# A 31-tap depthwise convolution bounced through DRAM: written and read back in pairs of chunks, run five chunks behind its gates, with weight unit 5 loaded after it

## The chip, the cores and the metric

The kernel runs on one core of a Trainium2 chip. The metric is the device time of one execution in microseconds (us). All times below are from one profiled execution of the kernel before the change, or from its three timed runs.

## What is computed

Two small transformer stacks run one after the other on 256 tokens of width 1024: the first has a convolution block, an attention block and two MLPs, the second two attention blocks and two gated MLPs. Only the convolution block of the first stack is touched:

```python
def conformer_conv(h, w_pw1, b_pw1, w_dw, b_dw, ln_g, ln_b, w_pw2, b_pw2):
    u = h @ w_pw1 + b_pw1
    a, gate = jnp.split(u, 2, axis=-1)
    u = a * jax.nn.sigmoid(gate)
    u = jnp.pad(u, ((0, 0), (CONV_WIDTH - 1, 0), (0, 0)))
    u = lax.conv_general_dilated(u, w_dw[:, None, :], window_strides=(1,), padding='VALID',
                                 dimension_numbers=('NWC', 'WIO', 'NWC'),
                                 feature_group_count=D_MODEL) + b_dw
    u = jax.nn.silu(layer_norm(u, ln_g, ln_b))
    return u @ w_pw2 + b_pw2
```

Everything after it (`h = h + rms_norm(m)`, the MLP, and all later layers) depends on its result.

## The kernel before, in words

Features lie on the 128 partitions, so the width of 1024 is eight chunks of 128 features by 256 tokens. Every float32 product is made of three float16 ones (high by high, low by high, high by low). Weights come from DRAM in units of 2 MB (4096 float32 per partition) into two buffers, `staged` 0 and 1, even units in the one, odd units in the other. A unit has two halves. ScalarE (ACT) makes the high part of a half (`split`, line 1460, `w_hi`), then VectorE (DVE) the low part (`split`, line 2124, `w_lo`); a half is numbered g, so unit u has g = 2u and 2u + 1. The semaphore `lo_split` counts the halves done. Units 0 to 3 are pw1, 4 and 5 pw2, 6 to 13 the first MLP's first matrix. SyncE (SP) issues every load in a written order; a unit may be loaded once both halves of the unit two before it are split.

The convolution block runs as follows.

- **Gates.** TensorE (PE) makes for each chunk j two products of pw1, the value and the gate (`glu_chunk`, lines 678 to 680, 48 matmuls of 256 columns). They lie in pairs of PSUM banks. Banks 0 and 1 serve chunks 0, 3, 5 and 7, banks 2 and 3 serve 1, 4 and 6, and banks 4 and 5 chunk 2 alone; so chunk 5 may start only when DVE has drained chunk 3, chunk 6 when it has drained chunk 4, chunk 7 after chunk 5. DVE drains with `late_pair` (line 2380), builds packed taps (line 2387), makes the gated value (line 2400) and its low part (line 2404), and after chunks 0 to 3 splits one half of a unit of weights (line 2124). ACT makes the sigmoid (line 1631) and the high part (line 1637).
- **Bounce.** The convolution packs four taps into the contraction. For that, the gated chunk (high and low part side by side, 576 float16 per partition) is written to DRAM (`write_glu`, line 623) and read back four times, each time shifted by one more element, to other partitions (`spread_glu`, line 633: four DMAs of 143 KB, rows of 572 elements). Four buffers hold shifted chunks, two in `qT` and two in `kT`.
- **Convolution.** `conv_chunk` (line 959) is 96 matmuls with 32-column weights for each chunk. Chunk j - CONV_LAG is convolved after the gates of chunk j. ACT takes the result out (`conv_out`, line 1622).
- **Layer norm.** PE sums the chunks (`mean`, line 966), DVE subtracts the mean (line 2414), ACT squares (line 1652), PE sums by token (line 734), ACT takes the root (line 1654), DVE inverts (line 2417), and so on to SiLU and the parts of pw2's input.
- **pw2.** PE makes eight products in four banks. DVE drains each, squares it and adds the square (lines 2228, 2207, 2217; `into_m`), and splits halves 12 and 13 between them; ACT splits halves 12 to 14. When all eight are summed, PE forms the sum by token (line 734), the norm's root follows (line 1498), and the first MLP can begin.

SP's order in this part before the change: unit 2, unit 3, then for each chunk c the write of chunk c + 1 and the four reads of chunk c, with unit 4 behind the reads of chunk 4, unit 5 behind those of chunk 5, and units 6 and 7, the constants and the positions at the end.

Of the kernel before, what the change touches and what calls it, by code (L numbers as in the profile page):

```python
# [31 lines left out]
P = 128  # L32
# [18 lines left out]
CONV_LAG = 4  # L51
# [246 lines left out]
def conformer_mla_fox_dsa_moba_kernel(nc, w_stream, vec_dram, const_dram, x_dram, pos_dram, out_dram):  # L298
    with ExitStack() as ctx:
# [59 lines left out]
        def pack_weights(b):  # L359
# [6 lines left out]
        U_SIZE = PACK * U_ROW  # L366
        shifted = [b[:].rearrange("p c t -> p (c t)").bitcast(F16)[:, U_SIZE * i:U_SIZE * (i + 1)].rearrange(
            "p (r h t) -> p r h t", r=PACK, h=2) for b in (qT, kT) for i in range(2)]
        u_rows = nc.dram_tensor("u_rows", (DC, P, U_ROW), F16, kind="Internal").ap()
# [43 lines left out]
        u_shifted = [sem(f"u_shifted_{b}") for b in range(U_RING)]  # L413
# [171 lines left out]
        def _(sp):  # L585
# [34 lines left out]
            def write_glu(c):  # L620

                sp.wait_ge(u_lo_ready, c + 1)
                sp.dma_start(u_rows[c], glu_parts[:, c % U_RING, :, :].rearrange("p h t -> p (h t)")).then_inc(
                    u_written[c % 2], 16)

            def spread_glu(c):

                sp.wait_ge(u_written[c % 2], 16 * (c // 2 + 1))
                if c >= U_RING:
                    sp.wait_ge(conv_product, c - U_RING + 1)  # L630
                by_group = u_rows[c].rearrange("(r c) n -> c r n", r=PACK)
                for j in range(PACK):
                    sp.dma_start(shifted[c % U_RING].rearrange("p r h t -> p r (h t)")[CPART * j:CPART * j + CPART, :,
                                                                                       0:U_ROW - PACK],
                                 by_group[:, :, j:j + U_ROW - PACK]).then_inc(u_shifted[c % U_RING], 16)
# [7 lines left out]
            write_glu(0)  # L643
            for c in range(DC):
                if c + 1 < DC:
                    write_glu(c + 1)
                spread_glu(c)
                if c in (4, 5):
                    early_unit(c)
# [17 lines left out]
        def _(pe):  # L667
# [275 lines left out]
            def conv_chunk(c):  # L943

                b = 4 + c % 3
                pe.wait_ge(u_shifted[c % U_RING], SHIFTED * (c // U_RING + 1))
# [7 lines left out]
                u = shifted[c % U_RING]  # L954
# [499 lines left out]
        def _(act):  # L1454
# [172 lines left out]
            for j in range(DC):  # L1627
# [6 lines left out]
                if j >= U_RING:  # L1634

                    act.wait_ge(u_shifted[j - U_RING], SHIFTED)
# [8 lines left out]
            for c in range(DC - CONV_LAG - 1, DC):  # L1645
                if c < DC - 1:
                    split(2 * FIRST["pw2"] + c - (DC - CONV_LAG - 1))
# [1314 lines left out]
```

## Time and profile before

| | us |
|---|---|
| three timed runs, median (lowest, highest) | 1207.9 (1207.46, 1215.44) |
| the profiled execution, its own time | 1205.27 |
| its span (first to last instruction) | 1203.3 |
| PE busy | 1154.8 |
| DVE busy | 849.2 |
| ACT busy | 671.8 |

The span lies 2 us inside the execution's own time. The stages that the change touches lie between 28 and 124 us of the span; what follows them is some 1080 us in which PE is busy nearly all the time. A busy PE is not PE at its peak, since matmuls overlap: the time from one start to the next (0.11 us for 256 columns) counts, not the duration of one (0.27 us).

### The profile page before, as it was taken

How to read it: one execution, taken by the hardware profiler on the slowest of the kernel's cores; microseconds unless marked ns; L12 is line 12 of the kernel's file. 1: busy time of each engine (PE TensorE's matmuls, PEld its weight loads, DVE VectorE, ACT ScalarE, POOL GpSimd, SP SyncE). 2: the span in 40 equal slices, each digit the busy share in tenths (PEclk: the TensorE clock that was granted, in tenths of full speed). 3: DMA queues.
4: the chain of work that ended last, by engine and by line, in shares of the span. 5: the costliest groups of instructions: out<-in, count | busy, mean ns of one | idle time of the engine just before them, and what ended most of it. 6: DMA issues, size and time to landing. Idle time of an engine off the chain costs nothing.

```text
span 1203.3 us, 26382 instructions
## 1 busy us (share of the span) xinstructions
PE 1154.8 (96%) x10544; PEld 987.7 (82%) x10544; DVE 849.2 (71%) x1403; ACT 671.8 (56%) x1034; POOL 213.6 (18%) x166
## 2 busy tenths in 40 slices
PE   9989999999889999999999999999999999999997
PEld 7878788888767888888877678888887777888886
DVE  5846786754865877555687468888677665888775
ACT  6445576433656466533565476665655656666542
POOL 0000000000002000000031433554231333355400
PEclk9998999999999999999999999999999999999999
DMA  8592365555251355555232435554565334455352
GB/s 335 156 321 79 117 243 191 196 209 209 79 202 71 141 211 209 210 205 193 91 115 97 152 128 183 217 214 147 166 249 189 120 108 181 155 216 207 139 197 78
DMA packets 22394, 208.37 MB, mean 173 GB/s; under 512 B 2480, under 2 KB 9008, under 8 KB 9136
## 3 DMA queue, kind: packets, MB, share of 16 engines
q1 hardware_dynamic: 22320, 207.32, 47.9%
q8 instruction: 53, 0.87, 0.3%
q14 instruction: 21, 0.17, 0.0%
HBM read 205.09 MB, written 2.23 MB: 172 GB/s over the span
## 4 chain that ended last, share of the span: by engine, by line
PE 52%; issue 17%; DVE 12%; POOL 6%; ACT 6%; DMA 5%; SPq 0%; POOLq 0%; DVEq 0%; ACTq 0%
PE ps L678 12%; PE ps L680 12%; PE ps L679 12%; POOL tmp L2054 5%; DMA staged<-weights 5%; DVE w_lo L2124 4%; ACT w_hi L1460 2%; PE ps L959 2%; POOL probs L2063 1%; PE ps L689 1%; PE ps L691 1%; PE ps L690 1%; PE ps L862 1%; PE ps L734 1%; PE ps L885 1%
## 5 line engine op out<-in xcount | busy, mean ns | idle before, releaser
L1460 ACT ACTIVATE w_hi<-staged 128x2048 f16<-128x2048 f32 (+3 forms) x190 | 352.6, 1870 | 192.4 <-PE ps L680 149.6
L2124 DVE SCALAR_TENSOR_TENSOR w_lo<-staged,w_hi 128x2048 f16<-128x2048 f32 (+3 forms) x190 | 424.6, 2249 | 40.9 <-ACT w_hi L1460 40.7
L678 PE MATMUL ps<-f_hi,w_hi 128*128 128x256 f16 x1596 | 435.1, 273 | 5.8 <-ACT qT L1539 2.7
L679 PE MATMUL ps<-f_lo,w_hi 128*128 128x256 f16 x1596 | 435.0, 273 | 0.0
L680 PE MATMUL ps<-f_hi,w_lo 128*128 128x256 f16 x1596 | 435.0, 273 | 0.0
L678 PE MATMUL ps<-x_hi,w_hi 128*128 128x256 f16 x912 | 249.2, 273 | 4.4 <-DVE x_lo L2154 2.9
L680 PE MATMUL ps<-x_hi,w_lo 128*128 128x256 f16 x912 | 249.0, 273 | 0.0
L679 PE MATMUL ps<-x_lo,w_hi 128*128 128x256 f16 x912 | 248.9, 273 | 0.0
L678 PEld LDWEIGHTS ps<-f_hi,w_hi 128*128 128x128 f16 x1596 | 156.1, 98 | 26.7 <-issue 3.4
L679 PEld LDWEIGHTS ps<-f_lo,w_hi 128*128 128x128 f16 x1596 | 156.2, 98 | 18.4
L680 PEld LDWEIGHTS ps<-f_hi,w_lo 128*128 128x128 f16 x1596 | 156.2, 98 | 18.1
L2063 POOL TENSOR_TENSOR probs<-probs,peak 128x128 f32<-128x128 f32 x80 | 64.3, 833 | 485.0 <-DVE peak L2309 373.8
L2054 POOL TENSOR_TENSOR tmp<-tmp,stat 128x256 f32<-128x256 f32 x44 | 110.4, 2510 | 124.2 <-ACT tmp L1938 124.2
L678 PEld LDWEIGHTS ps<-x_hi,w_hi 128*128 128x128 f16 x912 | 89.7, 98 | 25.7 <-issue 8.4
L679 PEld LDWEIGHTS ps<-x_lo,w_hi 128*128 128x128 f16 x912 | 89.3, 98 | 12.1 <-issue 0.2
L680 PEld LDWEIGHTS ps<-x_hi,w_lo 128*128 128x128 f16 x912 | 89.3, 98 | 10.6
L2478 DVE TENSOR_SCALAR m<-ps 128x256 f32 (+1 forms) x16 | 6.8, 424 | 63.3 <-PE ps L680 54.4
L1922 ACT ACTIVATE tmp<-pad,vec 128x256 f32<-128x256 f32 x44 | 26.4, 599 | 38.0 <-DVE pad L2700 37.8
L2073 POOL TENSOR_TENSOR kT<-kT,stat 128x256 f32<-128x256 f32 x5 | 5.0, 997 | 231.8 <-ACT kT L1800 231.8
L2453 DVE SCALAR_TENSOR_TENSOR tmp<-ps,stat 128x256 f32<-128x256 f32 x64 | 26.6, 418 | 22.9 <-PE ps L680 21.9
L689 PE MATMUL ps<-x_hi,w_hi 128*128 128x256 f16 x144 | 39.4, 273 | 2.0 <-DVE x_lo L2148 2.0
L691 PE MATMUL ps<-x_hi,w_lo 128*128 128x256 f16 x144 | 39.2, 273 | 0.0
(309 smaller groups left out, 1586.5 us busy)
## 6 DMA issues: line engine op xcount, KB each, us to landing
staged<-weights SPq DMA_DIRECT2D x81, 2048.0 KB, 8.1
staged<-weights SPq DMA_DIRECT2D x16, 1408.0 KB, 6.2
staged<-weights SPq DMA_DIRECT2D x4, 1024.0 KB, 10.4
qT<-u_rows SPq DMA_DIRECT2D x16, 143.0 KB, 3.6
kT<-u_rows SPq DMA_DIRECT2D x16, 143.0 KB, 3.1
u_rows<-probs SPq DMA_DIRECT2D x8, 144.0 KB, 2.5
cst<-constants SPq DMA_DIRECT2D x1, 1031.5 KB, 9.7
h<-x_turned SPq DMA_DIRECT2D x1, 1024.0 KB, 7.3
```

Source lines behind the costliest of these rows:

```text
L678: pe.matmul(out, wh, xh[:, c, :], start=(c == 0), stop=False)
L679: pe.matmul(out, wh, xl[:, c, :], start=False, stop=False)
L680: last = pe.matmul(out, wl, xh[:, c, :], start=False, stop=(c == kc - 1))
L689: pe.matmul(out, wh, xh[:, c, :], start=(c == 0), stop=False)
L691: last = pe.matmul(out, wl, xh[:, c, :], start=False, stop=(c == kc - 1))
L959: last = pe.matmul(ps[CPART * r:CPART * r + CPART, b, 0:T], w[:, c, q, :, r], u[:, r, h, at], start=(q == 0 and n == 0), stop=(q == PACKS ...
L1460: act.activation(w_hi[:, s, o:o + n], staged[:, s, o:o + n], ACT.Copy, scale=SW).then_inc(hi_split, 1)
L1922: act.activation(tmp[:, j, :], pad[:, j, 0:T], ACT.Identity, bias=vec[:, bass.ds(i * 4 + (VCOL[f"b_cv_{layer}"] + n), 1)], scale=vec[:, ba ...
L2054: pool.tensor_tensor(tmp[:, j, :], tmp[:, j, :], LATE_SCALE, ALU.mult).then_inc(g_normed[layer], 1)
L2063: last = pool.tensor_tensor(probs[:, hd % 3, sl], probs[:, hd % 3, sl], peak[:, hd % 2, 6 + t:7 + t].to_broadcast([P, P * (t + 1)]), ALU.mult)
L2124: dve.scalar_tensor_tensor(w_lo[:, s, o:o + n], staged[:, s, o:o + n], SW, w_hi[:, s, o:o + n], ALU.mult, ALU.subtract).then_inc(lo_split, 1)
L2453: dve.scalar_tensor_tensor(tmp[:, n % 2, :], ps[:, hidden_bank(i, n), 0:T], 0.0, LATE_SCALE, ALU.max, ALU.mult).then_inc(drained[one], 1)
```

## The change

- One write carries two chunks, and one set of four reads carries two chunks, in rows twice as long (`PAIR_ROW`; reads of 1148 elements). There are two buffers, each of a pair, in place of four, each of a chunk.
- `CONV_LAG` is 5 in place of 4.
- Unit 4 is issued behind the reads of pair 1 (chunks 2 and 3), unit 5 behind the reads of pair 3 (the last).
- ACT writes over a gated chunk once the pair before in that place is written to DRAM; before, it waited until the chunk had been read back.
- ACT splits halves 8 and 9 between the takings-out of the convolution, half 10 after the last of them and ahead of the norm's squares, and half 11 ahead of pw2's halves 12 to 14. DVE splits half 10 after the mean is subtracted, and half 11 in `into_m` after the first product.

```diff
-CONV_LAG = 4
+CONV_LAG = 5
...
-        U_SIZE = PACK * U_ROW
-        shifted = [b[:].rearrange("p c t -> p (c t)").bitcast(F16)[:, U_SIZE * i:U_SIZE * (i + 1)].rearrange(
-            "p (r h t) -> p r h t", r=PACK, h=2) for b in (qT, kT) for i in range(2)]
-        u_rows = nc.dram_tensor("u_rows", (DC, P, U_ROW), F16, kind="Internal").ap()
+        PAIR_ROW = 2 * U_ROW
+        shifted = [b[:].rearrange("p c t -> p (c t)").bitcast(F16)[:, 0:PACK * PAIR_ROW].rearrange(
+            "p (r i h t) -> p r i h t", r=PACK, i=2, h=2) for b in (qT, kT)]
+        u_rows = nc.dram_tensor("u_rows", (DC // 2, P, PAIR_ROW), F16, kind="Internal").ap()
...
+            def write_glu(p):
+
+                sp.wait_ge(u_lo_ready, 2 * p + 2)
+                b = 2 * (p % 2)
+                sp.dma_start(u_rows[p], glu_parts[:, b:b + 2, :, :].rearrange("p b h t -> p (b h t)")).then_inc(
+                    u_written[p % 2], 16)
+
+            def spread_glu(p):
+
+                sp.wait_ge(u_written[p % 2], 16 * (p // 2 + 1))
+                if p >= 2:
+                    sp.wait_ge(conv_product, 2 * p - 2)
+                by_group = u_rows[p].rearrange("(r c) n -> c r n", r=PACK)
                 for j in range(PACK):
+                    sp.dma_start(shifted[p % 2].rearrange("p r i h t -> p r (i h t)")[CPART * j:CPART * j + CPART, :,
+                                                                                      0:PAIR_ROW - PACK],
+                                 by_group[:, :, j:j + PAIR_ROW - PACK]).then_inc(u_shifted[p % 2], 16)
...
-            write_glu(0)
-            for c in range(DC):
-                if c + 1 < DC:
-                    write_glu(c + 1)
-                spread_glu(c)
-                if c in (4, 5):
-                    early_unit(c)
+            for p in range(DC // 2):
+                write_glu(p)
+                spread_glu(p)
+                if p % 2:
+                    early_unit(4 + p // 2)
             early_unit(6)
             early_unit(7)
...
-                pe.wait_ge(u_shifted[c % U_RING], SHIFTED * (c // U_RING + 1))
+                pe.wait_ge(u_shifted[c // 2 % 2], SHIFTED * (c // 4 + 1))
...
-                    act.wait_ge(u_shifted[j - U_RING], SHIFTED)
+                    act.wait_ge(u_written[j // 2 % 2], 16)
...
             for c in range(DC - CONV_LAG - 1, DC):
-                if c < DC - 1:
-                    split(2 * FIRST["pw2"] + c - (DC - CONV_LAG - 1))
+                if c < 4:
+
+                    act.wait_ge(product["pw1"], 2 * c + 8)
+                    split(2 * FIRST["pw2"] + c - 2)
                 conv_out(c)
+            split(2 * FIRST["pw2"] + 2)
             root_next()
...
+            split(2 * FIRST["pw2"] + 3)
             behind("pw2")
...
+                    if name == "pw2" and n == 0:
+                        split(2 * u0 + 3)
                     if n % 2 and n < DC // 2:
                         split(2 * u0 + n // 2 + 4)
...
-            for g in range(4):
+            for g in range(2):
                 split(2 * FIRST["pw2"] + g)
...
+            split(2 * FIRST["pw2"] + 2)
             dve.wait_ge(ln_rooted, 1)
```

The change moves instructions on PE, ACT and DVE; three places follow, each first before the change and then with it (line numbers of the changed kernel are one to five off). A name in brackets is a semaphore that the row waits for.

The first is PE's row at the end of chunk 4's gates (678 to 680, in the changed kernel 677 to 679, are gates; 959, or 958, is the convolution). Before:

```order
L679 MATMUL ps<-x_lo,w_hi 128x256
L680 MATMUL ps<-x_hi,w_lo 128x256
L959 MATMUL ps<-qT,f_hi 32x256 [waits pw1_drained,pack_built,u_shifted_0]
L959 MATMUL ps<-qT,f_hi 32x256 x7
L959 MATMUL ps<-qT,f_lo 32x256 x4
```

And with the change:

```order
L678 MATMUL ps<-x_lo,w_hi 128x256
L679 MATMUL ps<-x_hi,w_lo 128x256
L677 MATMUL ps<-x_hi,w_hi 128x256 [waits pw1_drained,lo_split]
L678 MATMUL ps<-x_lo,w_hi 128x256
L679 MATMUL ps<-x_hi,w_lo 128x256
```

Where the convolution of chunk 0 stood, the gates of chunk 5 stand now; their first matmul waits for a drained bank and for a split half, and the convolution comes 48 matmuls later.

The second is ACT's row from the convolution's takings-out (1622, now 1621) to the norm's squares (1652, now 1654); 1460 (now 1459) is the high part of a half of weights. Before:

```order
L1622 ACTIVATE xn<-ps,vec 128x256 [waits conv_product]
L1460 ACTIVATE w_hi<-staged 128x2048 [waits landed_1]
L1622 ACTIVATE xn<-ps,vec 128x256 [waits conv_product]
L1460 ACTIVATE w_hi<-staged 128x2048 [waits landed_1]
L1622 ACTIVATE xn<-ps,vec 128x256 [waits conv_product] x2
L1528 ACT_TABLE_LOAD
L1528 ACTIVATE unused<-cst 128x1
L1652 ACTIVATE sq<-xn 128x256 [waits ln_centred] x8
```

And with the change:

```order
L1459 ACTIVATE w_hi<-staged 128x2048 [waits landed_0,pw1_product]
L1621 ACTIVATE xn<-ps,vec 128x256 [waits conv_product] x5
L1459 ACTIVATE w_hi<-staged 128x2048 [waits landed_1]
L1527 ACT_TABLE_LOAD
L1527 ACTIVATE unused<-cst 128x1
L1654 ACTIVATE sq<-xn 128x256 [waits ln_centred] x8
```

Half 10 has moved from between the takings-out to behind the last one, ahead of the table load and the squares.

The third is DVE's row at the start of `into_m`. Before (2228, 2207 and 2217 are drain, square and sum of one product, 2124 is the low part of a half):

```order
L2228 TENSOR_SCALAR m<-ps,vec 128x256
L2207 TENSOR_TENSOR sq<-m 128x256
L2217 TENSOR_TENSOR stat<-stat,sq 128x256
L2228 TENSOR_SCALAR m<-ps,vec 128x256
L2207 TENSOR_TENSOR sq<-m 128x256
L2217 TENSOR_TENSOR stat<-stat,sq 128x256
L2124 SCALAR_TENSOR_TENSOR w_lo<-staged,w_hi 128x2048
```

And with the change:

```order
L2231 TENSOR_SCALAR m<-ps,vec 128x256 [waits pw2_product,dve_step]
L2210 TENSOR_TENSOR sq<-m 128x256 [waits pw2_drained]
L2220 TENSOR_TENSOR stat<-stat,sq 128x256 [waits m_squared]
L2127 SCALAR_TENSOR_TENSOR w_lo<-staged,w_hi 128x2048 [waits hi_split]
L2231 TENSOR_SCALAR m<-ps,vec 128x256 [waits pw2_product]
L2210 TENSOR_TENSOR sq<-m 128x256 [waits pw2_drained]
L2220 TENSOR_TENSOR stat<-stat,sq 128x256 [waits m_added,m_squared]
L2127 SCALAR_TENSOR_TENSOR w_lo<-staged,w_hi 128x2048 [waits hi_split]
```

One half more (number 11) is split there, between the first product and the second; two others stand in both kernels.

## Rows read from the trace of the kernel before

**Rows 1.** The page, busy us, share of the span and instructions of an engine.

```profile
PE 1154.8 (96%) x10544; PEld 987.7 (82%) x10544; DVE 849.2 (71%) x1403; ACT 671.8 (56%) x1034; POOL 213.6 (18%) x166
```

**Rows 2.** Stretches (us): PE, PEld, DVE, ACT, POOL busy (instructions), PEclk, DMA share, GB/s.

```profile
72.00:74.00 2.00, 1.47 (x29) 1.32 (x32) 2.00 (x2) 0.00 (x0) 0.00 (x0) 0.50 0.91 330
74.00:76.00 2.00, 2.00 (x60) 1.89 (x53) 0.34 (x1) 0.44 (x1) 0.00 (x0) 0.70 0.92 174
...
69.70:78.50 8.80, 4.95 (x128) 4.43 (x127) 4.49 (x2) 4.43 (x5) 0.00 (x0) 0.81 0.77 245
...
41.30:44.10 2.80, 2.75 (x96) 2.55 (x96) 2.80 (x4) 1.55 (x2) 0.00 (x0) 1.00 0.64 180
```

**Rows 3.** Timeline of PE: start, duration (us), [idle before, releaser].

```profile
34.17 0.27 PE L678 MATMUL ps<-x_hi,w_hi 128*128 128x256 f16 x1 [0.32 <-DVE tmp L2380]
41.35 0.42 PE L959 MATMUL ps<-qT,f_hi 128*32 128x256 f16 x8 [1.78 <-DMA qT<-u_rows]
...
57.54 0.42 PE L959 MATMUL ps<-kT,f_hi 128*32 128x256 f16 x8
...
65.64 0.42 PE L959 MATMUL ps<-kT,f_hi 128*32 128x256 f16 x8
...
72.53 0.41 PE L959 MATMUL ps<-qT,f_hi 128*32 128x256 f16 x3 [2.88 <-issue]
...
78.94 0.41 PE L959 MATMUL ps<-qT,f_hi 128*32 128x256 f16 x7 [1.46 <-issue]
...
87.02 1.99 PE L966 MATMUL ps<-xn,cst 128*128 128x256 f32 x8
```

**Rows 4.** Timeline of DVE in the gates: drains of chunks 1, 3, 4; a split.

```profile
33.61 0.74 DVE L2380 TENSOR_TENSOR tmp<-ps,stat 128x256 f32<-128x256 f32 x2
...
41.00 2.28 DVE L2124 SCALAR_TENSOR_TENSOR w_lo<-staged,w_hi 128x2048 f16<-128x2048 f32 x1
43.21 0.74 DVE L2380 TENSOR_TENSOR tmp<-ps,stat 128x256 f32<-128x256 f32 x2
...
48.01 0.74 DVE L2380 TENSOR_TENSOR tmp<-ps,stat 128x256 f32<-128x256 f32 x2
```

**Rows 5.** DMA in stretches, KB each and us to landing.

```profile
u_rows<-probs SPq DMA_DIRECT2D x1, 144.0 KB, 1.7
...
u_rows<-probs SPq DMA_DIRECT2D x1, 144.0 KB, 8.9
...
staged<-weights SPq DMA_DIRECT2D x1, 2048.0 KB, 14.5
...
staged<-weights SPq DMA_DIRECT2D x1, 2048.0 KB, 8.0
...
q8 instruction: 1, 0.02, 6.9%
```

**Rows 6.** The page, DMA issues of the whole span, median us to landing.

```profile
kT<-u_rows SPq DMA_DIRECT2D x16, 143.0 KB, 3.1
```

**Rows 7.** Timeline of SP: the bounce's last write and last four reads.

```profile
68.13 0.34 SPq L623 DMA_DIRECT2D u_rows<-probs  x1
...
77.06 1.88 SPq L633 DMA_DIRECT2D kT<-u_rows  x4
```

**Rows 8.** Timeline of ACT behind the convolution's last taking-out.

```profile
87.64 1.28 ACT L1528 ACT_TABLE_LOAD   x1
...
89.51 2.73 ACT L1652 ACTIVATE sq<-xn 128x256 f32<-128x256 f32 x8 [0.38 <-DVE xn L2414]
...
107.24 1.91 ACT L1460 ACTIVATE w_hi<-staged 128x2048 f16<-128x2048 f32 x1 [3.48 <-PE ps L691]
```

**Rows 9.** Timelines of DVE and PE in pw2: first drain, last sum, PE behind it.

```profile
106.98 0.48 DVE L2228 TENSOR_SCALAR m<-ps,vec 128x256 f32<-128x256 f32 x1 [2.47 <-PE ps L691]
...
120.24 0.43 DVE L2217 TENSOR_TENSOR stat<-stat,sq 128x256 f32<-128x256 f32 x1
...
120.81 0.58 PE L734 MATMUL ps<-cst,stat 128*128 128x1 f32 x4 [0.19 <-DVE stat L2217]
```

More of the change, by code:

```diff
@@ L411, in conformer_mla_fox_dsa_moba_kernel @@
         u_lo_ready = sem("u_lo_ready")
-        u_shifted = [sem(f"u_shifted_{b}") for b in range(U_RING)]
+        u_shifted = [sem(f"u_shifted_{b}") for b in range(2)]
         conv_product = sem("conv_product")
@@ L618, in stream @@
                     unit(0, end - 1)
[L620 to L631, printed above, removed]
+            def write_glu(p):
[8 more added lines that the diff above has]
+                by_group = u_rows[p].rearrange("(r c) n -> c r n", r=PACK)
                 for j in range(PACK):
-                    sp.dma_start(shifted[c % U_RING].rearrange("p r h t -> p r (h t)")[CPART * j:CPART * j + CPART, :,
-                                                                                       0:U_ROW - PACK],
-                                 by_group[:, :, j:j + U_ROW - PACK]).then_inc(u_shifted[c % U_RING], 16)
+                    sp.dma_start(shifted[p % 2].rearrange("p r i h t -> p r (i h t)")[CPART * j:CPART * j + CPART, :,
+                                                                                      0:PAIR_ROW - PACK],
+                                 by_group[:, :, j:j + PAIR_ROW - PACK]).then_inc(u_shifted[p % 2], 16)
             def early_unit(u):
@@ L953, in conv_chunk @@
                     pe.wait_ge(conv_ready, c - 2)
-                u = shifted[c % U_RING]
+                u = shifted[c // 2 % 2]
                 for q in range(PACKS):
@@ L958, in conv_chunk @@
                         for r in range(PACK):
-                            last = pe.matmul(ps[CPART * r:CPART * r + CPART, b, 0:T], w[:, c, q, :, r], u[:, r, h, at],
+                            last = pe.matmul(ps[CPART * r:CPART * r + CPART, b, 0:T], w[:, c, q, :, r], u[:, r, c % 2, h, at],
                                              start=(q == 0 and n == 0), stop=(q == PACKS - 1 and n == 2))
```

## The prediction, made before the changed kernel ran

> **What bounds the kernel now.** I read the page first: PE is busy for 1154.8 of 1203.3 us [rows 1], so time is won or lost where PE stands still or runs at a lower clock. The bounce through DRAM lies between 28 and 90 us, so I read PE's timeline there and looked for idle time in brackets [rows 3]. The reader is to see four places. PE waits 0.32 us for DVE's drain at 34.17; 1.78 us for the first shifted chunk, at 41.35; and twice for nothing that the profile names ("issue"), 2.88 us before 72.53 and 1.46 us before 78.94, both inside a run of convolution matmuls. The windows [rows 2] add that PE's granted clock is 0.50 (1.2 GHz) in 72 to 74 and 0.70 on average in 74 to 76, so the 2.88 us pause is followed by a slow stretch, while the pause of 1.78 us is not (clock 1.00 in 41.30 to 44.10). Last I read DVE, the DMA queue and ACT for what would be late next.
>
> The unit price: conv to conv is 65.64 - 57.54 = 8.10 us [rows 3]; one convolution of 96 matmuls is 2.75 us [rows 2]; so the gates of a chunk are 5.3 us. Four means are 2.0 us [rows 3].
>
> The "issue" pauses: exactly 128 matmuls lie between the first and the second (window 69.70 to 78.50 [rows 2]), and the 6.9% of a microsecond on 16 engines in [rows 5] is one instruction packet that moved in 70 to 71. I read them as PE running out of instructions: a back-to-back convolution eats 128 matmuls in 128/96 x 2.75 = 3.7 us, while the queues are full of unit 5, which needed 14.5 us to land where a lone unit needs 8.0, and of the bounce, whose write took 8.9 us where a free one takes 1.7 [rows 5].
>
> **The change part by part.**
>
> (a) *The lag.* The gates of chunk 5 now follow those of chunk 4 at once. PE is ready at 41.35 - 1.78 = 39.57. But banks 0 and 1 hold chunk 3, and DVE drains chunk 3 only at 43.21 [rows 4]. DVE does not stand still in that stretch: it is at 4.8 us a chunk, 2.28 of them a split of weights (chunks 3 and 4 at 43.21 and 48.01 [rows 4]), and nothing in the change makes it earlier. PE starts 34.17 - 33.61 = 0.56 us after a drain starts [rows 3, 4]: at 43.77. So the wait of 1.78 us goes, and one of 4.20 takes its place: +2.4 us. Queued behind it on PE are the convolutions and with them ACT's takings-out. Every later input of the gates is in time (chunk 4 drained at 48.6 for gates 6).
>
> (b) *The clock after it.* A pause of 2.88 us was followed by half clock until about 75, that is 2.6 us of work at half speed, 1.3 us lost; a pause of 1.78 lost nothing [rows 2]. 4.20 lies beyond the first: I take +1.3 (bounds 0, and 2.5 for a slow stretch twice as long).
>
> So PE runs: gates 5 from 43.8 to 50.4 (slow start in it), conv 0 to 53.1, gates 6 to 58.4, conv 1 to 61.2, gates 7 to 66.4, conv 2 to 69.2, conv 3 to 71.9, conv 4 to 74.7, conv 5 to 77.4, if nothing else stops it.
>
> (c) *The bounce in pairs.* Reads of pairs 0, 1 and 2 are in by about 44, 54 and 67 (write 1.7 to 2.7, reads 1.9 and 3.1 behind the later chunk's low part, or behind conv 1) for use at 50.4, 66.4 and 71.9: free. Pair 3 is tight. Chunk 7's low part is out 2.5 us after gates 7, as before (65.64 and 68.13 [rows 3, 7]), at 68.9; the write lands by 71.5; the reads must wait for conv 3, so they are issued at 72.0 and take 1.88 us to issue [rows 7] and 3.1 to land [rows 6]. Twice the bytes in as many packets costs between nothing (the packet is the price) and 2 us (the byte is); I take 1.5. That is 78.5, against 77.4 at which PE wants it: +1.1.
>
> (d) *Weights behind the bounce.* Unit 4 is issued at 50.5, unit 5 at 74.0. No unit is on the way in 61 to 74, so the pause at 69.65 should go with its slow stretch: -2.9 - 1.3. The next block of instructions is asked for at about 73 and used up at 76.7. It meets the reads and unit 5 behind them, as the reads issued until 78.94 [rows 7] met unit 6, where no third pause followed, or as the block did that was asked for at about 66 and brought a pause of 2.88 [rows 3]. I take about 1 us, and it lies beside the wait of (c), which it mostly hides: together 1.6 us, so conv 6 starts at 79.0. Conv 6, four means and conv 7 are 7.45 us: the convolution ends at 86.4, where it was 87.0 [rows 3]. (a) to (d) together: -0.6 us (bounds -3.4, no slow clock and no wait, and +3.5, both pauses as they were).
>
> (e) *Half 10 on ACT ahead of the squares.* Before, ACT loaded its table at 87.64 (1.28 us), was then 0.38 us early, and squared from 89.51, 2.5 us after the convolution's end at 87.02 [rows 3, 8]. Unit 5 has landed by then (74 + 8 to 10). Half 10 is 1.91 [rows 8] less that 0.38: +1.5 us for the squares, and PE's sums by token, the root and all behind it. PE, whose means end 2.0 us after the convolution, is also idle for some 2 us there in place of 0.5, so its sums may start at the lower clock: 0 to 0.6, I take 0.4. DVE's half 10 (2.28) lies between subtraction and the reciprocal, in time in which DVE waits for the sums: free. If I am wrong there the price is 2.3 at most.
>
> (f) *Half 11 in pw2.* ACT's part lies before 107.24, in its wait of 3.48 [rows 8]: free. DVE's does not. DVE works without a gap from its first drain at 106.98 to its last sum's end at 120.67, and PE, done at 120.81 - 0.19 = 120.62, waits for it [rows 9]. A split is 2.2 us from its start to the next instruction's (41.00 to 43.21 [rows 4]), and it is added in full. PE's banks are still drained in time (each at least 1 us early), so its products don't slip: +2.2. Before, DVE did this half in the convolution, in idle time.
>
> (g) *Unit 7* may be loaded only once half 11 is split, in pw2, where before it was loaded during the means. It lands 8.0 us later [rows 5], and ACT's half 14, table load and last square then end within 0.3 us of (f)'s end: 0, but up to +2 if the load takes 10.
>
> Sum: -0.6 + 1.5 + 0.4 + 2.2 = +3.5 us on the profiled 1205.3, that is 1208.8. The runs shown have a median 2.6 us above that execution, so the measured time is 1207.9 + 3.5 = 1211.4. Behind 124 us nothing changes, so the difference stays as it is to the end.
>
> A rule that speaks against (d): "DMA: Bandwidth & Descriptors" of the Trainium skill, in the section on queues, rings and completion order, says that each DMA engine takes turns between its queues at packet granularity. By it an instruction packet never waits behind a whole unit of weights, and moving unit 5 would save none of the pauses; in this trace the pauses do fall where weights and bounce share the queues, which leans against it but doesn't decide. Its consequence is rival 2.
>
> **The rivals.**
>
> 1. *The bounce's relief is larger than its price: not slower.* The place is the run of convolutions. If the clock doesn't fall at 43.8, no block of instructions is late and the reads of pair 3 are in time, the convolution ends at 83.6, 3.4 us early, and ACT's and DVE's halves (+3.7 to +4.1) are paid back but for half a microsecond: 1208.2; with half 11 finding a gap on DVE (-1 to -2.2) 1206 to 1207. For it: the pauses fall where a unit of weights is under way, and it is moved. Against it: DVE's drain at 43.21 is fixed. It decides if the convolution ends before 83.
>
> 2. *PE's pauses stay.* Blocks are late because four convolutions back to back need one every 3.7 us, with or without weights. Then both pauses and the slow stretch (2.9 + 1.5 + 1.3 = 5.7) stay, in place of 1.6: +4.1, 1215.5. For it: with a lag of 5, five convolutions run one behind another (2 to 6), where before it was four. Against it: the first packet came only in the full queues.
>
> 3. *pw2 hangs on unit 7*, (g) at its worst: +2, 1213.4. For it: a unit in company takes 9 us and more. Against it: nothing else is in the queues then.
>
> 4. *The change does not do what it says*: pairs 2 and 3 wait for products so that the bounce is no shorter; it is within (c), and the time is that of the forecast.
>
> **How the numbers follow.** My forecast has 0.5 (it ends between 1209 and 1213.5), rival 1 0.25, rival 2 0.15, rival 3 0.08, something else 0.02. Range: the lower end takes in rival 1 to its middle and 0.3% of spread between runs, 1204.5; the upper end takes in rivals 2 and 3 up to 1216. Faster or slower by over 1% (12 us), about what a measurement can tell from no change, needs a mechanism that no row shows: 0.01 and 0.02. All the cases above lie within it, 0.97.
>
> **What would show each step.** (a) A wait of PE at the gates of chunk 5 for DVE's drain of about 4.2 us, ending near 43.8. (b) A granted clock of 0.50 around 44 to 46. (c, d) At most a short pause after the fourth convolution in a row; writes that land in under 3 us; the last convolution's end near 86.4. (e) Squares that begin 4 us after that end. (f) DVE without a gap through pw2 and PE waiting some 2.3 us for its last sum. Wrong would be: gates 5 starting by 42, a convolution that ends before 83 or after 90, or a last sum in pw2 that PE does not wait for.

## The result, and the profile after

The changed kernel takes 1214.35 us in the median of 11 runs (1211.01 to 1219.49); the kernel before took 1204.96 on the same chip (11 runs, 1203.09 to 1215.98). The ratio is 1.0065 with a 95% interval from 1.0036 to 1.0094: about 7.8 us slower, between 4.3 and 11.3. It lies inside 1%, where the forecast was, and the sign is the forecast's, but it is about twice the +3.5 us. The profiled execution took 1216.66 us, 2.3 more than the median, and its span of 1214.8 us is 11.5 longer than the span before; the ratio, not these two single executions, is the measure of the size.

Of the page's first two parts (busy times as in [rows 1]; granted clock in 40 slices of the span, in tenths):

```profile
PE 1160.6 (96%) x10544; PEld 991.7 (82%) x10544; DVE 849.2 (70%) x1403; ACT 671.3 (55%) x1034; POOL 213.8 (18%) x166
PEclk9988899999999999999999999999999999999999
```

As many PE instructions as before take 5.8 us longer (1160.6 against 1154.8). The slices 3 to 5 (61 to 152 us) of the granted clock stand at 8; in the kernel before it is one slice, the fourth (90 to 120 us):

```profile
PEclk9998999999999999999999999999999999999999
```

So part of the loss is work at the lower clock. The rest of the 11.5 us is more standing still.

PE's timeline after, from the first wait to the first MLP, as in [rows 3, 9] (start, busy, ..., and in brackets the idle time before and what ended it). Line 958 is the convolution, 965 the mean, 733 a sum by token, and 836 warm-up matmuls, whose results nobody reads:

```profile
44.29 0.27 PE L677 MATMUL ps<-x_hi,w_hi 128*128 128x256 f16 x1 [3.61 <-DVE tmp L2385]
...
81.42 0.62 PE L958 MATMUL ps<-kT,f_hi 128*32 128x256 f16 x8 [4.46 <-DMA kT<-u_rows]
...
91.42 1.99 PE L965 MATMUL ps<-xn,cst 128*128 128x256 f32 x8
95.69 5.73 PE L733 MATMUL ps<-cst,sq 128*128 128x1 f32 x32 [2.27 <-ACT sq L1654]
101.97 1.23 PE L741 MATMUL ps<-cst,root_col 128*128 128x128 f32 x4 [0.55 <-DVE root_col L2423]
102.99 3.62 PE L836 MATMUL ps<-decay_k 128*128 128x256 f32 x8
...
130.38 0.58 PE L733 MATMUL ps<-cst,stat 128*128 128x1 f32 x4 [2.40 <-DVE stat L2220]
132.07 1.22 PE L741 MATMUL ps<-cst,root_col 128*128 128x128 f32 x4 [0.62 <-DVE root_col L2144]
```

The reader is to see three things. Both "issue" pauses of [rows 3] are gone. Three waits stand in their place: 3.61 us for DVE's drain, 4.46 for the last pair's reads, 2.40 for the last sum in pw2. And the convolution ends at 91.42 where it ended at 87.02.

SP's queue says why the reads are late (start and time to issue; compare [rows 7]):

```profile
63.09 1.75 SPq L634 DMA_DIRECT2D qT<-u_rows  x4
68.31 0.34 SPq L624 DMA_DIRECT2D u_rows<-probs  x1
72.48 2.73 SPq L634 DMA_DIRECT2D kT<-u_rows  x4
75.25 43.06 SPq L640 DMA_DIRECT2D staged<-weights  x3
```

and the issues of DMAs of the whole page give the medians to landing, in us, last in the row (of a single chunk's reads [rows 6]):

```profile
qT<-u_rows SPq DMA_DIRECT2D x8, 287.0 KB, 4.8
kT<-u_rows SPq DMA_DIRECT2D x8, 287.0 KB, 5.7
```

Pair 3's write starts at 68.31, while pair 2's reads are still landing (the DMA share is 1.03 until 70), and takes 72.48 - 68.31 = 4.2 us. Its reads are all in at 81.4, 8.9 us after the first was issued. A part of that is SP's own: the four reads take 2.73 us to issue where pair 2's took 1.75, and of the four one alone takes 1.43 us where their median is 0.43. No run here shows why that one is slow.

The windows (stretch, its length, busy time and count of PE, weight loads, DVE, ACT, POOL, then granted clock, DMA share, GB/s):

```profile
69.00:70.00 1.00, 1.00 (x46) 1.00 (x42) 0.01 (x1) 1.00 (x2) 0.00 (x0) 1.00 1.03 260
70.00:71.00 1.00, 1.00 (x48) 1.00 (x42) 1.00 (x1) 1.00 (x2) 0.00 (x0) 1.00 0.26 95
```

```profile
42.00:44.00 2.00, 0.00 (x0) 0.00 (x0) 2.00 (x2) 0.92 (x1) 0.00 (x0) 1.00 1.03 219
44.00:46.00 2.00, 1.71 (x16) 1.56 (x17) 2.00 (x6) 0.93 (x2) 0.00 (x0) 1.00 0.56 103
...
80.00:82.00 2.00, 0.58 (x12) 0.45 (x16) 0.00 (x0) 0.00 (x0) 0.00 (x0) 0.51 1.00 404
82.00:84.00 2.00, 2.00 (x48) 1.41 (x40) 0.00 (x0) 0.00 (x0) 0.00 (x0) 0.50 1.05 442
84.00:88.00 4.00, 4.00 (x58) 2.85 (x51) 0.00 (x0) 0.47 (x1) 0.00 (x0) 0.64 0.96 410
98.00:100.00 2.00, 2.00 (x11) 2.00 (x11) 0.40 (x1) 0.00 (x0) 0.00 (x0) 0.50 0.03 8
134.00:138.00 4.00, 4.00 (x15) 2.84 (x14) 3.45 (x9) 2.44 (x6) 0.00 (x0) 0.50 0.00 0
```

After the wait that ends at 44.29 the clock stays at 1.00. In the wait that ends at 81.42 the clock falls (0.51 in 80 to 82); it is 0.50 to 84 and 0.64 on average in 84 to 88. After the wait in pw2 it is 0.50 until 138, where before it was 1.00 (122 to 138 in that trace). There PE's wait of 2.40 us is followed by about 2 us of lost work (the next list), nearly its own length.

DVE and ACT in the norm and in pw2, as in [rows 8, 9]:

```profile
93.84 1.28 ACT L1527 ACT_TABLE_LOAD   x1
95.24 2.54 ACT L1654 ACTIVATE sq<-xn 128x256 f32<-128x256 f32 x8
...
101.46 0.26 ACT L1656 ACTIVATE root_col<-ps,cst 128x2 f32<-128x2 f32 x1 [3.68 <-PE ps L733]
```

```profile
114.34 0.48 DVE L2231 TENSOR_SCALAR m<-ps,vec 128x256 f32<-128x256 f32 x1 [3.33 <-PE ps L690]
...
115.67 2.28 DVE L2127 SCALAR_TENSOR_TENSOR w_lo<-staged,w_hi 128x2048 f16<-128x2048 f32 x1
```

The squares start 3.8 us after the convolution's end, where it was 2.5. DVE's first drain in pw2 starts at 114.34, half 11 follows at 115.67 (2.28 us), and its last sum ends at 130.24: 15.9 us without a gap, where it was 13.7.

How the delay grows (after less before, by the start of the same instruction, in these two executions): DVE's drain of chunk 3 0.5 (43.73 against 43.21 [rows 4]); end of the convolution 4.4; squares 5.7; root 6.5; first drain in pw2 7.4; PE's last sum 9.6; the norm in the first MLP 11.6; end of the span 11.5. Behind 150 us nothing is added.

### The profile page after: what moved, and what is told of

Same layout as the page of the kernel before. It is cut to its first block, busy times and chain, and to the rows that moved or that the text cites. A ratio compares the mean times of both kernels' runs of the same rounds, so it can differ in the third digit from the quotient of the medians.

```text
span 1214.8 us, 26362 instructions
## 1 busy us (share of the span) xinstructions
PE 1160.6 (96%) x10544; PEld 991.7 (82%) x10544; DVE 849.2 (70%) x1403; ACT 671.3 (55%) x1034; POOL 213.8 (18%) x166
## 4 chain that ended last, share of the span: by engine, by line
PE 53%; issue 16%; DVE 13%; POOL 6%; ACT 6%; DMA 4%; POOLq 0%; SPq 0%; DVEq 0%; ACTq 0%
PE ps L677 13%; PE ps L678 12%; PE ps L679 12%; POOL tmp L2057 5%; DVE w_lo L2127 4%; DMA staged<-weights 3%; ACT w_hi L1459 2%; POOL probs L2066 1%; PE ps L688 1%; PE ps L690 1%; PE ps L689 1%; PE ps L958 1%; PE ps L733 1%; PE ps L861 1%; PE ps L884 1%
## 5 line engine op out<-in xcount | busy, mean ns | idle before, releaser
L679 PE MATMUL ps<-x_hi,w_lo 128*128 128x256 f16 x912 | 248.9, 273 | 0.0
L678 PE MATMUL ps<-x_lo,w_hi 128*128 128x256 f16 x912 | 248.8, 273 | 0.0
L689 PE MATMUL ps<-x_lo,w_hi 128*128 128x256 f16 x144 | 40.5, 281 | 0.0
```

Of the source, the lines that this page charges most:

```text
L678: pe.matmul(out, wh, xl[:, c, :], start=False, stop=False)
L679: last = pe.matmul(out, wl, xh[:, c, :], start=False, stop=(c == kc - 1))
L689: pe.matmul(out, wh, xl[:, c, :], start=False, stop=False)
```

## The experiments

Twelve runs, in three sets (e1 to e4, e5 to e8, e9 to e12); each set has runs of the kernel before on its own chip (medians 1211.15, 1206.38 and 1207.55). e1 to e6 were timed four times each, the others ten or twelve times; the intervals of the first set reach 5 to 8 us to each side. Names of theories are those of each expectation's own text. All ratios are to the kernel before.

### e1: the lag alone

```diff
-CONV_LAG = 4
+CONV_LAG = 5
```

(ACT's splits stay at the same chunks.)

> The kernel before with the lag alone (five chunks in place of four; bounce, rows and loads as before). Theory: PE waits some 3.6 to 4.2 us for DVE's drain of chunk 3 in place of 1.78 us for the bounce, and five convolutions in a row keep both instruction pauses: +2 to +4 us against the kernel before. Rival (the lag is what pays, since the bounce is late for PE): no slower, 0 to -2 us.

1210.55 us, ratio 1.0007 [0.9944, 1.0069]. PE's timeline and its window behind the wait:

```profile
43.82 0.27 PE L678 MATMUL ps<-x_hi,w_hi 128*128 128x256 f16 x1 [4.20 <-DVE tmp L2380]
```

```profile
44.00:46.00 2.00, 2.00 (x15) 1.58 (x14) 2.00 (x6) 0.64 (x2) 0.00 (x0) 0.71 0.59 132
```

The wait is that of (a), 4.20 us ending at 43.8, to the row. Here the clock behind it falls (0.71), as (b) says. The "issue" pauses shrink to 1.88 and 0.30 us, and the convolution ends at 88.24, 1.2 us later than before. With four timings the interval reaches from 7 us faster to 8 us slower, so the time decides neither for the theory (+2 to +4 us) nor for its rival; the trace shows the theory's wait, and pauses that shrink but stay.

### e2: the pairs alone

Pairs as in the change, but lag 4, units 4 and 5 both behind pair 2's reads, splits as before. So the pairs aren't quite alone here: pair 3's write and reads queue behind two units.

```diff
-                if p % 2:
-                    early_unit(4 + p // 2)
+                if p == 2:
+                    early_unit(4)
+                    early_unit(5)
```

> The change's pairs alone: lag of four, units 4 and 5 behind the reads of pair 2 together, halves 10 and 11 split where they were. Theory: the first convolution waits for pair 0's reads until about 45.5 (+4 us), and pair 3's write and reads queue behind two units: the last two convolutions wait until about 90, +8 to +12 us in all. Rival (the pairs cost nothing, fewer packets make up for it): 0 to +4 us.

1217.3 us, ratio 1.0062 [1.0012, 1.0111], or 1.5 to 13 us, which includes the theory's 8 to 12 and not all of the rival's 0 to 4. The issue of pair 0's reads on SP, then PE's timeline:

```profile
38.37 1.76 SPq L634 DMA_DIRECT2D qT<-u_rows  x4
```

```profile
45.87 0.62 PE L959 MATMUL ps<-qT,f_hi 128*32 128x256 f16 x8 [6.35 <-DMA qT<-u_rows]
...
88.12 0.62 PE L959 MATMUL ps<-kT,f_hi 128*32 128x256 f16 x8 [5.47 <-DMA kT<-u_rows]
```

With a lag of 4, the first convolution waits 6.35 us for the first pair, and the seventh 5.47 us for the last. Pair 0's reads have nothing else in the queues and still take 45.87 - 38.37 = 7.5 us from the first issue to the last landing; the prediction had 6.5 for a pair. The convolution ends at 97.17, 10.1 us late. Here the pairs, with the two units ahead of the last one, are the costly part, and the lag of 5 is what hides the first of them. How much of the 5.47 us is the units was not separated. The "issue" pauses are 1.39 and 0.30 us, so pairs do not remove them by themselves.

### e3, e4, e8: the places of the weights alone

e3 is the kernel before with unit 5 behind chunk 7's reads and the splits as in the change:

```diff
-                if c in (4, 5):
-                    early_unit(c)
+                if c in (4, DC - 1):
+                    early_unit(4 + c // 7)
```

> The kernel before with unit 5 behind the last reads, and halves 10 and 11 split where the change splits them; chunks and lag as before. Theory (PE's pauses come from unit 5 sharing the queues with the bounce): no pause of over 1 us in the convolutions, which end some 4 to 5 us earlier; the splits cost 3.5 and up to 2 more by a lower clock: -1 to +1 us. Rival (the pauses have nothing to do with unit 5, since instruction packets take turns with it): both pauses stay, and the kernel is 3.5 to 5 us slower.

1212.17 us, ratio 1.0012 [0.9958, 1.0067]. PE's timeline:

```profile
74.38 0.41 PE L959 MATMUL ps<-qT,f_hi 128*32 128x256 f16 x7 [0.37 <-issue]
...
82.45 1.99 PE L966 MATMUL ps<-xn,cst 128*128 128x256 f32 x8
87.95 5.67 PE L734 MATMUL ps<-cst,sq 128*128 128x1 f32 x32 [3.51 <-ACT sq L1653]
...
122.65 0.58 PE L734 MATMUL ps<-cst,stat 128*128 128x1 f32 x4 [2.39 <-DVE stat L2219]
```

The pauses fall from 4.34 to 0.37 us, and the convolution ends 4.6 us earlier. But half 10 on ACT waits for unit 5 (1.12 us) and the squares behind it, and DVE's half 11 makes PE's last wait in pw2 2.39 us, where it was 0.19: the last sum is 1.8 us later than before. So in this trace (e) and (f) eat (d)'s gain whole. The interval is too wide to say so of the time.

e4 is e3 with half 10 on ACT behind the squares and half 11 on DVE ahead of its first step in pw2, places where both stand idle (at least in part, see e7); e8 moves half 10 between the fourth and fifth square:

```diff
-            split(2 * FIRST["pw2"] + 2)
             root_next()
...
+            split(2 * FIRST["pw2"] + 2)
             act.wait_ge(ln_summed, 2)
...
-                    if name == "pw2" and n == 0:
-                        split(2 * u0 + 3)
...
+            split(2 * FIRST["pw2"] + 3)
             into_m("pw2", "mix_post_0")
```

> The same as e3, but half 10 is split on ACT behind the norm's squares and half 11 on DVE ahead of pw2's drains. Theory: half 10 lies in ACT's wait for the sums (2.7 us) and half 11 mostly in DVE's wait for pw2's first product (2.5 us), so 3 to 4 us come back against e3: 1198 to 1202 us where the kernel before has 1205, faster than both. Rival (the splits were not on the path): the same time as e3.

> e4 again (chunks and lag of before, unit 5 behind the last reads, splits in gaps), with half 10 on ACT between the fourth and the fifth square, so that DVE's half 10 ends before the root. Theory: without instruction pauses of over 1.5 us the convolution ends 3 to 4.5 us earlier than before, and the end of pw2 1.5 to 3 us earlier: 0.1 to 0.3% faster than the kernel before, faster than the change by 0.7 to 0.9%. Rival (the low clock around the norm eats it): the same as before.

e4: 1207.8 us, 0.9975 [0.9927, 1.0023]; e8: 1205.94 us, 1.0000 [0.9977, 1.0024]. e4's last sum:

```profile
119.75 0.58 PE L734 MATMUL ps<-cst,stat 128*128 128x1 f32 x4 [0.47 <-DVE stat L2219]
```

The wait in pw2 shrinks from 2.39 to 0.47 us, which is (f) by itself. The ratio of e4 includes 1, so that it is faster than the kernel before, as its theory said, is not shown; for e8 the rival (the same as before) holds. In e8 the convolution ends at 82.20, 4.8 us early, and the last sum is at 118.94, only 1.9 us early: between them the clock is 0.63 in 86 to 88 and 0.50 from 88 to 96, where in the kernel before it was 1.00 until 92 and low until 99.

### e5, e6: what makes the last pair's reads late

e5 is the change with unit 5 held back until all of the last pair's reads have landed:

```diff
+                if p == 3:
+                    sp.wait_ge(u_shifted[1], 2 * SHIFTED)
                 if p % 2:
                     early_unit(4 + p // 2)
```

e6 is the change with each pair's read cut in eight DMAs of 143 KB with rows half as long.

> The changed kernel, with unit 5 held back until pair 3's four reads have landed. Theory A (the reads are late because unit 5 follows them into the same queues): from issue to the last landing they take about 6.6 us, as pair 0's did alone, in place of 8.9, PE's wait before the convolution of chunk 6 falls from 4.5 to about 2.2 us, and the convolution ends 2 to 3.5 us earlier; unit 5 then lands near 88 to 90, about when ACT wants it, so 1 to 3 us of it stay in the end. Theory B (twice the bytes in rows twice as long is all of it): the wait stays at 4 us or more.

> The changed kernel, with each read of a pair cut in two reads of the old row length (572 elements, eight DMAs of 143 KB for a pair). Theory A (the price is the bytes and unit 5's company, not the length of a row): pair 0's reads, from the first issue to the last landing, take 6.5 to 7.5 us, as in the change, and the wait for pair 3 stays within 1.5 us of 4.5. Theory C (long rows move badly): 5 to 6 us for pair 0, and a wait of under 3 us for pair 3.

e5: 1216.46 us, ratio 1.0088 [1.0059, 1.0118]; e6: 1217.78 us, ratio 1.0095 [1.0066, 1.0124]. SP's queue and PE's timeline of e5:

```profile
72.25 2.50 SPq L634 DMA_DIRECT2D kT<-u_rows  x4
80.44 36.40 SPq L640 DMA_DIRECT2D staged<-weights  x3
```

```profile
80.46 0.42 PE L960 MATMUL ps<-kT,f_hi 128*32 128x256 f16 x8 [3.27 <-DMA kT<-u_rows]
...
87.89 1.99 PE L967 MATMUL ps<-xn,cst 128*128 128x256 f32 x8
92.91 6.98 PE L735 MATMUL ps<-cst,sq 128*128 128x1 f32 x32 [3.04 <-ACT sq L1656]
```

With nothing behind them, the reads still take 80.44 - 72.25 = 8.2 us, of which 2.50 are SP's issue, again with one slow issue. Neither expectation is met: PE's wait of 3.27 us lies between theory A's 2.2 and theory B's 4. Unit 5 in the same queues costs the reads at most the other 0.7. In e6 PE waits 4.86 us:

```profile
82.33 0.62 PE L960 MATMUL ps<-kT,f_hi 128*32 128x256 f16 x8 [4.86 <-DMA kT<-u_rows]
```

Shorter rows don't help either, as theory A of e6 has it. What is left is mostly the amount, four reads of 287 KB, 1.15 MB: of the 8.9 us, 7.5 are those of a pair alone (e2), about 0.7 SP's slow issue and about 0.7 unit 5's company. As an estimate from these rows this holds; no run took the slow issue away. The convolution ends 3.5 us earlier than in the change, and the time is no better (the two intervals overlap): unit 5 is now issued 5.2 us later, half 10 ahead of the squares waits 0.65 us for it, and the sums by token take 6.98 us at the lower clock where they took 5.73 in the change.

### e7: the change with the splits in the gaps

The edit of e4 on the changed kernel.

> The changed kernel, with half 10 split on ACT behind the norm's squares and half 11 on DVE ahead of pw2's drains. Theory: squares begin 2.5 us after the convolution's end in place of 3.8, PE's last wait in pw2 is 0.2 to 0.5 us in place of 2.4, and the low clock behind that wait goes: 3.5 to 5.5 us less than the changed kernel. Rival (the two splits were not on the path): the same time as the change.

1212.43 us, ratio 1.0044 [1.0024, 1.0064]. The last sum waits 1.60 us in place of 2.40:

```profile
126.55 0.58 PE L733 MATMUL ps<-cst,stat 128*128 128x1 f32 x4 [1.60 <-DVE stat L2220]
```

By the ratios about a third of the loss was the two splits, but the interval overlaps the change's (1.0036 to 1.0094); in the traces the last sum starts 3.8 us earlier than in the change. The late reads stay (3.47 us of waiting). The splits did not become free: the squares begin 2.5 us after the convolution's end, as expected, but DVE's half 10 now ends just before the reciprocal, and PE waits 2.14 us for the inverted root where it waited 0.55; and DVE goes from half 11 straight to its first drain, without idle time, so the last wait is 1.60 us and not 0.2 to 0.5. The clock is 0.50 behind it all the same (128 to 133).

### e9, e10: each pair read back in two halves

The write stays one of a pair; the reads of the earlier chunk go first and have their own semaphore.

```diff
-                for j in range(PACK):
+                for i, j in [(i, j) for i in range(2) for j in range(PACK)]:
...
-                                 by_group[:, :, j:j + PAIR_ROW - PACK]).then_inc(u_shifted[p % 2], 16)
+                                 by_group[:, :, U_ROW * i + j:U_ROW * (i + 1) + j - PACK]).then_inc(
+                        u_shifted[2 * (p % 2) + i], 16)
...
-                pe.wait_ge(u_shifted[c // 2 % 2], SHIFTED * (c // 4 + 1))
+                pe.wait_ge(u_shifted[c % 4], SHIFTED * (c // 4 + 1))
```

e10 is e9 with the splits of e4.

> The changed kernel, but each pair is read back as two halves of one chunk each (eight DMAs of 143 KB, all of the earlier chunk's four first), each half with a semaphore of its own; the write stays one of a pair. Theory A (the bytes set the price: 1.15 MB of a pair at some 200 GB/s, behind which the sixth convolution waits although it needs only half of them): chunk 6's half is in some 3 to 4 us earlier, so PE's wait of 4.46 us at 81.4 falls to 0 to 2 us and the convolution ends 2 to 4.5 us earlier than the change's 91.4, at 87 to 89.5; time 2 to 4 us under the change. Rival C (the reads wait for what is in the queues ahead of them, the write and the reads of pair 2, and not for their own bytes): the wait stays at 3.5 or more.

> The run before, with half 10 on ACT behind the squares and half 11 on DVE ahead of its first step in pw2, where both engines stand idle. The bounce's and the splits' prices taken away together: if these two are all of the change's loss, the time is within 2 us of the kernel before; if a clock that stays low behind PE's new waits is a term of its own, PE's sums and warm-up matmuls are still at 0.50 and 2 us or more of the loss stay.

e9: 1214.18 us, ratio 1.0057 [1.0033, 1.0081]; e10: 1206.25 us, ratio 0.9997 [0.9969, 1.0025]. PE's timeline of e9, then of e10:

```profile
79.42 0.42 PE L959 MATMUL ps<-kT,f_hi 128*32 128x256 f16 x8 [1.06 <-DMA kT<-u_rows]
...
86.85 1.99 PE L966 MATMUL ps<-xn,cst 128*128 128x256 f32 x8
92.89 6.98 PE L734 MATMUL ps<-cst,sq 128*128 128x1 f32 x32 [4.04 <-ACT sq L1655]
...
129.22 0.58 PE L734 MATMUL ps<-cst,stat 128*128 128x1 f32 x4 [2.39 <-DVE stat L2221]
```

```profile
77.89 0.42 PE L959 MATMUL ps<-kT,f_hi 128*32 128x256 f16 x8 [0.38 <-DMA kT<-u_rows]
...
88.28 3.78 PE L734 MATMUL ps<-cst,sq 128*128 128x1 f32 x32 [0.96 <-ACT sq L1654]
94.79 1.23 PE L742 MATMUL ps<-cst,root_col 128*128 128x128 f32 x4 [2.73 <-DVE root_col L2422]
...
121.34 0.58 PE L734 MATMUL ps<-cst,stat 128*128 128x1 f32 x4 [1.27 <-DVE stat L2221]
```

The wait of 4.46 us is 1.06 and 0.38 us: half of the bytes are in 79.42 - 73.87 = 5.6 us after their first issue (e9), where all of them took 8.9, so the seventh convolution had waited for the eighth's bytes. That shows the pair's own bytes as the main cause of the wait (theory A; rival C expected 3.5 or more). But e9 is only about 1 us better than the change (1.0057 against 1.0065, with overlapping intervals, where theory A expected 2 to 4). In the trace eight reads take 4.9 us to issue, unit 5 starts 3.6 us later, half 10 on ACT, ahead of the squares, now waits 1.66 us for it, and the sums take 6.98 us at the lower clock. With half 10 behind the squares, and half 11 in DVE's idle time, the loss is gone: 0.9997, within the 2 us that e10's expectation gives to these two prices alone (the interval reaches 3.7 us). The clock still falls there (0.50 in 92 to 98, as in the kernel before), but behind the sums, which take 3.78 us. So the warm-up matmuls still run at 0.50 as the other reading of that expectation has it, but the 2 us of loss that it goes with did not stay. The two prices are not a sum: the last sum in pw2 starts 1.2 us (e9), 3.8 us (e7) and 9.0 us (e10) earlier than in the change. Each covers the other, and only both taken away give the time back.

### e11, e12: does the clock eat the lead of e8?

e12 is e8 once more; e11 adds three warm-up matmuls of PE to it, two ahead of the 32 sums by token and one in their middle. The third stands behind the wait for the fifth square, so it does not fill PE's idle time there, as its expectation says it would, but follows it.

```diff
+            keep_warm(2, 0)
             for c in range(DC):
                 pe.wait_ge(ln_squared, c + 1)
+                if c == 4:
+                    keep_warm(1, 0)
```

> The run e8 (kernel before with the new places of the weights and of halves 10 and 11) with two warm-up matmuls of PE ahead of the 32 sums by token and one in their middle, in PE's idle time there. Theory L (the convolution's 4.8 us are given back because PE idles and sums single columns there, so that its clock falls earlier): the clock stays at 1.00 for longer, the 32 sums take 5 us or less from first to last, the time is 1 to 3 us below the run e8 of this call. Rival: the clock falls in the sums all the same and the three matmuls (0.4 us each at the full clock, 0.9 at half) are added or hidden: within 1 us of e8, or above it.

> The run e8 once more, the reference for the run before it: 1205 to 1208 on a chip on which the kernel before takes 1206, that is, no difference that can be measured; if the convolution's lead of 4.8 us reached the end, it would be 1201.

e11: 1206.33 us, ratio 0.9992 [0.9971, 1.0012]; e12: 1204.65 us, ratio 0.9981 [0.9960, 1.0002]. PE's third warm-up in e11:

```profile
90.34 1.22 PE L837 MATMUL ps<-decay_k 128*128 128x256 f32 x2 [1.15 <-ACT sq L1655]
```

In e11 the clock is 1.00 to 90 and 0.51 from there, so it fell in the 1.15 us of idle time before this matmul, which then runs at the lower clock; the sums last from 87.24 to 94.8, 7.5 us, against 5.7 in e12. The rival's outcome came: the clock falls there all the same, and the time is not under e12's. That a warm-up inside the idle time would not have held the clock is not shown. The lead of the convolution in e12 is 2.3 us, as its pauses came back (1.51, 0.57 and 1.15 us of "issue"), so the pauses also differ between executions of one kernel.

The traces of e12 and of the kernel before part a second time, in attention, which no edit touches. Both windows, before first:

```profile
352.00:364.00 12.00, 10.48 (x57) 6.92 (x57) 4.96 (x18) 6.52 (x20) 1.04 (x3) 1.00 0.06 27
```

```profile
352.00:364.00 12.00, 10.61 (x37) 6.34 (x38) 3.92 (x11) 4.30 (x10) 0.00 (x0) 0.61 0.10 42
```

From ACT's table load at 353 to the next one it is 35.4 us in the kernel before and in the change, 36.9 in e2, 37.0 in e5 and e6, 39.9 in e8, e9, e10 and e12, and 45.8 in e1, whose clock in 352 to 364 is 0.64. An execution draws 0 to 10 us more in this stage, so two single spans can differ by that much without any edit, and edits of 2 or 3 us have to be read in the ratio or in the starts of instructions ahead of this stage. No version is faster than the kernel before by more than its interval.

## Why the prediction was right or wrong

The difference is under 1% and slower, as forecast, and the range (1204.5 to 1216.0) held the time, but the sum was half of what was measured. The forecast's own stretch, 1209 to 1213.5, did not hold 1214.35; rival 3's 1213.4 and rival 2's 1215.5 lie nearer than the forecast, and neither of their mechanisms came about. That the time itself is only 2.9 us over the forecast 1211.4 is in part luck: the sum was set on a median before of 1207.9, which eleven runs put at 1204.96; from there it gives 1208.5, 5.9 us too little. And by the prediction's own list of what would be wrong, a convolution that ends after 90, it was wrong in (c): the end is 91.42.

(a), the lag: right. The forecast start was 43.77, and it is 44.29 in the change (DVE's drain itself starts 0.5 us later there), 43.82, 43.30 and 43.63 in e1, e5 and e10.

(b), the clock after it: not in the change's own trace (1.00), where the sum had +1.3 us for it. But e1 shows 0.71 in 44 to 46, e5 0.62, e6 0.50, e7 and e9 0.79 and e10 0.51, and in e1, e5, e7 and e10 the low clock lasts 3 to 4 us, so 1.5 to 2 us are lost. The step held as a chance, not as a certainty.

(c), the bounce in pairs: this step failed, and it failed in size, by the bytes' price and by what was put at nothing. I took 3.1 us to land plus 1.5 for twice the bytes in as many packets, and a write that lands in 2.5 us. Measured: the write 4.2, and 8.9 us from the first read's issue to the last landing where I had 6.5. The end I called "the byte is the price" (+2 us) was nearer, and still too small: a pair alone takes 7.5 us (e2), +2.5. The rest of the 8.9 is the slow issue and unit 5, about 0.7 us each (e5). I had not asked whether pair 2's reads, issued at 63.09, would be out of the queues when the write of pair 3 came; that made the write late, but the reads' issue only by 0.5 us (72.48 instead of 72.0), as they also had to wait for the fourth convolution. Reads at 81.4 instead of 78.5, and PE ready at 77.0, make the wait of 4.46 us. e9 shows that most of it is the pair's own bytes. The convolution ended 3.9 us late beyond the start's 0.5, where (a) to (d) gave -0.6 (added up from their terms, +2.4 + 1.3 + 1.6 less 4.34 + 1.3, they give -0.3).

(d), the pauses: they go, as forecast, and even the 1 us that I had left for one does not appear. There is none in the change or in e5, e6, e7, e9 and e10. With unit 5 not moved they are 2.18 us in e1 and 1.69 in e2, against 4.34 in the one trace of the kernel before. With the weights moved alone the pauses are 0.37 us in e3, 0.31 in e8 and none in e11, but 2.3 in e4 and 3.2 in e12; whether it is the weights, the halved packets or the lag that removes them surely is open.

(e), half 10: right, 1.33 us where I had 1.5, and 0.76 where I had 0.4 for the sums at the lower clock. (f), half 11: right, 2.21 where I had 2.2. (g), unit 7: ACT's half 14 does wait for it, but DVE's sum is last, as forecast.

Left out of the sum: the lower clock behind the waits that the change itself makes. I counted it for (a) and for the sums by token, but not behind the wait of (c), where 82 to 84 stands at 0.50 (the convolution from 81.42 to 91.42 takes 10.0 us where it needs 7.45, so 2.5 us), nor for pw2's warm-up (+0.9) and for the stretch behind (f)'s wait (+2.0). These are 5.4 us of the 8.0 by which this trace's 11.5 us exceed the forecast 3.5; the others are mainly the longer wait in (c) (+2.9, less the 1.3 of (b) that did not come) and the later start (0.5). The ratio's 7.8 us is a smaller figure than the two traces' 11.5, so the terms are worth less in the median, and how much less is open. That the +2.0 is the price of (f)'s wait is argued: in e4 a wait of only 0.47 us is followed by a clock of 0.58 in 122 to 126.

The rivals. Rival 1, the larger relief: e3, e4, e8, e11 and e12 show that the relief exists without the pairs (2.3 to 4.8 us in the convolution), but it does not reach the end. Rival 2, pauses that stay: not in this kernel. The trace of the change has none; the pauses were 4.34 us in sum with unit 5 in the bounce's queues and 0.37 in e3, where it was moved. The Trainium skill ("DMA: Bandwidth & Descriptors", on queues, rings and completion order) lets each engine take turns between its queues packet by packet, by which moving the unit would have saved nothing; e3 speaks against that, and the 2.3 and 3.2 us of e4 and e12 keep it from being settled. Rival 3 did not come about (DVE's sum, not ACT's half 14, is last). Rival 4 did not in its form either: the pairs' bounce is not shorter, it is longer, and that is outside (c) as I had priced it.

## What to carry to other kernels

When transfers are joined, the first user waits for the bytes of the last: price a joined read by its bytes at the rate of the nearest row, and ask what is still in the queue when it starts. For every wait that a change makes on PE, add the stretch behind it at the lower clock; here it cost 2.5 us behind a wait of 4.46, about 2 behind one of 2.40, and nothing behind one of 3.61. And look what stands behind the repaired place before counting its worth: here late reads and a split of weights covered each other, each repair alone was worth 1 to 2.5 us by the ratios (not clear of noise), and both together 8.

## What the runs showed of the hardware

- Reads of 287 KB with rows of twice the length moved no faster for their bytes: four of them, 1.15 MB, with a median of 5.7 us from issue to landing, some 200 GB/s; a single chunk's four, 0.57 MB, take 3.1 us [rows 6], some 185 GB/s (both are estimates, bytes over the median). Cut in twice as many (e6) they landed no earlier and 0.9 us later. By these medians twice the bytes took nearly twice the time.
- The granted clock after a stop of PE is not given by the stop's length: 1.00 behind 3.61 us in the change, 0.79 in 44 to 46 behind 3.61 in e7 and e9, 0.50 from 82 to 84 behind 4.46 us, and 0.58 in 122 to 126 behind 0.47 us in e4, but 1.00 behind 3.27 us in e5 and behind 1.78 in [rows 3]. Behind 4.20 us it fell in all four kernels that had that wait (e1, e5, e6, e10).
- The clock also falls while PE is not idle: within the 32 sums of a single column by token, in the kernel before (it is 1.00 to 92 and 0.56 in 92 to 94, with PE busy for the whole 2 us), in e8 and in e12. In e11 it fell in a pause of 1.15 us in their middle, with two full matmuls ahead of the sums and one behind the pause.
- In an untouched stage (353 to 389 us) the same code took 35.4, 37, 39.9 or 45.8 us, with the clock at 1.00 or, in e1 and e12, at 0.64 and 0.61 in 352 to 364: the spread of the runs (1203.09 to 1215.98 for the kernel before) is of that size.
